# Moving taps of a convolution and chunks of a weight matrix about a block of attention steps

## The reference, cut to what matters

```python
q, k, v, qi, ki, wi, glu = jnp.split(rmsnorm(x, norm_mix_g) @ w_in, cuts, axis=-1)
a_out = dsa_attention(q, k, v, qi, ki, wi)      # 8 heads, 4 query blocks of 128, top-128 keys by an index score
ga, gg = jnp.split(glu, 2, axis=-1)
u = ga * jax.nn.sigmoid(gg)                     # 512 channels
u = causal_dwconv(u, conv_b_w, conv_b_b)        # 31 taps for each channel
b_out = jax.nn.silu(layernorm(u, ln_b_g, ln_b_b))
x = x + jnp.concatenate([a_out, b_out], axis=-1) @ w_out
m = rmsnorm(mem, norm_mem_g)                    # 256 memory rows
kc, vc = m @ w_k_cross, m @ w_v_cross           # keys and values of the later cross attention
```

## Time and profile before

| what | value |
|---|---|
| median of 3 runs | 1393.65 us (1391.83 to 1396.83) |
| time of the profiled execution | 1390.86 us |
| its span on the core | 1388.7 us |
| PE busy | 1337.5 us (96%) |
| DVE / ACT / POOL busy | 786.7 / 543.4 / 611.7 us |
| granted TensorE clock, mean | 0.99 |

### The profile page before, as it was taken

How to read it: one execution, slowest core, us unless ns; L and a number is a source line. 1 busy time by engine, 2 the same in 40 slices (tenths; PEclk the granted TensorE clock), 3 DMA queues, 4 the chain that set the end, 5 groups by cost and what they waited for, 6 DMA issues and landing times.

```text
span 1388.7 us, 18012 instructions
## 1 busy us (share of the span) xinstructions
PE 1337.5 (96%) x6189; PEld 1083.1 (78%) x6189; DVE 786.7 (57%) x1100; ACT 543.4 (39%) x855; POOL 611.7 (44%) x299
## 2 busy tenths in 40 slices
PE   7998989999999999999999998899999999999997
PEld 5787867787678888888888777677778888888887
DVE  6697897643456777777534588666453333332231
ACT  5454676543243322322223353444442322323322
POOL 4587974432244444444434533122344444444341
PEclk9999999999999999999999999899999999999999
DMA  6122321221122323223332222111122323223322
GB/s 224 46 91 90 114 70 47 76 92 61 46 76 92 105 91 98 98 91 108 104 104 79 89 78 74 46 47 46 61 91 93 104 91 101 95 96 106 103 84 82
DMA packets 31875, 121.19 MB, mean 87 GB/s; under 512 B 3536, under 2 KB 3664, under 8 KB 31568
## 3 DMA queue, kind: packets, MB, share of 16 engines
q1 hardware_dynamic: 31392, 119.55, 25.9%
q10 hardware_dynamic: 432, 0.96, 0.3%
HBM read 118.40 MB, written 2.10 MB: 87 GB/s over the span
## 4 chain that ended last, share of the span: by engine, by line
PE 73%; issue 13%; POOL 5%; DVE 5%; ACT 3%; DMA 1%; POOLq 0%; SPq 0%; ACTq 0%; DVEq 0%
PE acc L1701 60%; POOL weights_low L610 4%; PE acc L1838 3%; PE aux L2090 1%; PE acc L2186 1%; POOL conv L659 1%; PE aux L2070 1%; PE acc L1810 1%; DVE aux L1206 1%; PE aux L1924 1%; ACT weights_high L689 1%; DVE left L1551 1%; PE aux L2080 1%; DVE a_low L1367 1%; DMA weights_raw<-w 1%
## 5 line engine op out<-in xcount | busy, mean ns | idle before, releaser
L610 POOL TENSOR_TENSOR weights_low<-weights_raw,weights_high 128x1024 fp32r<-128x1024 f32 (+1 forms) x204 | 526.1, 2579 | 743.7 <-ACT weights_high L689 741.3
L689 ACT CAST weights_high<-weights_raw 128x1024 fp32r<-128x1024 f32 (+1 forms) x202 | 222.0, 1099 | 507.2 <-PE acc L1701 480.1
L1701 PE MATMUL acc<-a_high,weights_high 128*128 128x512 f32 x976 | 389.8, 399 | 4.5 <-POOL weights_low L610 3.1
L1701 PE MATMUL acc<-a_high,weights_low 128*128 128x512 f32 x976 | 381.1, 390 | 0.0
L1701 PE MATMUL acc<-a_low,weights_high 128*128 128x512 f32 x976 | 380.6, 390 | 0.0
L1701 PEld LDWEIGHTS acc<-a_high,weights_high 128*128 128x128 f32 x976 | 183.7, 188 | 47.0 <-issue 6.4
L1701 PEld LDWEIGHTS acc<-a_low,weights_high 128*128 128x128 f32 x976 | 183.8, 188 | 39.6 <-issue 2.6
L1701 PEld LDWEIGHTS acc<-a_high,weights_low 128*128 128x128 f32 x976 | 183.6, 188 | 38.5
L1179 DVE TENSOR_TENSOR residual<-acc,residual 128x512 f32<-128x512 f32 (+1 forms) x63 | 43.3, 687 | 172.0 <-PE acc L1701 129.8
L1701 PE MATMUL acc<-h_high,weights_high 128*128 128x512 f32 x330 | 129.0, 391 | 0.0
L1701 PE MATMUL acc<-h_high,weights_low 128*128 128x512 f32 x330 | 128.5, 389 | 0.0
(11 more groups left out here) (378 smaller groups left out, 1933.2 us busy)
## 6 DMA issues: line engine op xcount, KB each, us to landing
weights_raw<-w SPq DMA_DIRECT2D x172, 512.0 KB, 3.3
weights_raw<-w SPq DMA_DIRECT2D x32, 704.0 KB, 4.1
residual<-xT SPq DMA_DIRECT2D x8, 256.0 KB, 7.6
out<-y_tok SPq DMA_DIRECT2D x4, 512.0 KB, 3.1
mem_raw<-memT SPq DMA_DIRECT2D x1, 1024.0 KB, 5.4
mem_tok<-mem SPq DMA_DIRECT2D x1, 1024.0 KB, 7.4
lru_weights<-blockdiag ACTq DMA_DIRECT2D x1, 512.0 KB, 3.4
sine<-positions ACTq DMA_DIRECT2D x1, 256.0 KB, 7.0
```

Of the source, the lines that this page charges most:

```text
L610: g.tensor_tensor(weights_low[:, s, 0:cols], weights_raw[:, s, 0:cols], weights_high[:, s, 0:cols].bitcast(F32), ALU.subtract).then_inc(we ...
L689: a.copy(weights_high[:, s, 0:cols], weights_raw[:, s, 0:cols]).then_inc(weight_high, 1)
L1701: last = t_.matmul(acc[:, bank, 0:cols], w[:, s, wide], x_[:, k0 + k, 0:cols], start=start and k == opens and n == 0, stop=stop and k == c ...
```

## The change

No instruction is added or taken away; the same items stand in another order in `FIRST_PLAN`:

```diff
+        for n, first, end in ((12, 0, 2), (13, 2, 4), (14, 4, 7), (15, 7, 10)):
+            BETWEEN[n] += [("tap", i) for i in range(first, end)]
...
-        FILLS_AT = (2, 1, 2, 1, 2, 1, 2, 1, 1, 1, 2, 1, 1, 1, 1, 1, 1, 1, 0, 1, 1, 0, 1, 0,
-                    1, 0, 1, 0, 0, 1, 0, 0, 1, 0, 1)
-        CONV_STEPS, PRODUCT_STEPS = 31, 30
+        FILLS, HELD = FILLS[:23], FILLS[23:]
+        FILLS_AT = (1, 1, 1, 1, 1, 1, 1, 1, 1, 1, 1, 1, 1, 1, 1, 1, 1, 0, 1, 0, 1, 0, 1, 0,
+                    1, 0, 0, 1, 0, 0, 1, 0, 0, 0, 0)
+        LATE_TAPS = 12
+        CONV_STEPS, PRODUCT_STEPS = 33, 32
...
             if step < CONV_STEPS:
-                FIRST_PLAN += [("tap", i) for i in range(step * len(CONV) // CONV_STEPS,
-                                                         (step + 1) * len(CONV) // CONV_STEPS)]
+                rest = len(CONV) - 10 - LATE_TAPS
+                FIRST_PLAN += [("tap", 10 + i) for i in range(step * rest // CONV_STEPS,
+                                                              (step + 1) * rest // CONV_STEPS)]
...
-        FIRST_PLAN += [("mean",), ("heads_out", 3), ("centre",)] + FIRST[:2] + [("squares",)] + FIRST[2:4]
+        FIRST_PLAN += HELD[:2] + [("heads_out", 3)]
+        for n, item in enumerate(HELD[2:]):
+            FIRST_PLAN += [item] + [("tap", len(CONV) - LATE_TAPS + 2 * n + i) for i in range(2)]
+        FIRST_PLAN += [("mean",), ("centre",)] + FIRST[:2] + [("squares",)] + FIRST[2:4]
```

## The result

The changed kernel takes 1403.5 us in the median of 4 runs (1401.76 to 1405.56), the kernel before 1392.74 in 4 (1391.27 to 1396.83). The ratio is 1.0067, 95% interval 1.0051 to 1.0082: slower by 7.1 to 11.4 us. The profiled execution is the one of 1405.56 us. In it everything ahead of the change is already 1.5 us later than in the profile before (`glu 2` ends at 108.06, not 106.55). The two kernels are the same up to there. PE waits 2.8 us for a `weights_low` early on in both, and behind that wait the clock stays up in one profile and falls in the other.

The account below looks back on a forecast made before the run. The prediction saw DVE and PE waiting for each other, DVE giving the pace, and the front bound by when DVE reaches mask 0. It summed 9.2 − 14.3 + 13.7 = +8.6 us to 1402 us, range 1396 to 1408.5.

Parts of the forecast that it names:

- B: First to last mask: fewer halves and taps, so 81.8 us instead of 96.07, a gain of 14.3 us.
- C: Last mask to first half of w_out: held halves and taps make it 23.8 us instead of 10.1, +13.7 us.
- A, the taps ahead: Before the first mask: tap 0 waits 7.9 us for glu 2, so mask 0 comes 9.2 us later.
- with DVE giving the pace: First to last mask, kernel before: DVE, busy 84.16 of 96.07 us, and PE wait for each other; DVE paces.
- The rule weighed: PE waits in the tail: the page's throttling at each gap gives +10.2 us; the 1.66 us row, no clock loss, +8.6.
- Rival 1: First to last mask at PE's floor, 75.8 us: sum +2.6 us, 1396 us, no change that shows; chance 0.12.
- Rival 2: Steps wait as much as before, 86.4 us, and the tail's clock slows: +14.9 us, 1408.5 us; chance 0.18.
- Rival 3: Before the first mask: glu 2 ready for tap 0, mask 0 at 133.4, sum +0.8 us, 1394.5 us; chance 0.08.

Follow-up runs that it names:

- Experiment 4: Changed kernel with its first four taps moved ahead of the rotation of query 2: 1399.61 us against 1394.10 for the kernel before, ratio 1.0029.
- Experiment 1: Kernel before with only ten taps put ahead of the steps, the other 74 in the steps: 1402.81 us against 1394.10, ratio 1.0057.
- experiment 9: Kernel before with its 31 halves one in each of steps 0 to 30, no tap moved, nothing held: 1386.58 us against 1394.19, ratio 0.9943.
- 6: Changed kernel with heads_out 3 before the held chunks, five taps ahead where DVE idles: 1389.20 us against 1393.77 for the kernel before, ratio 0.9962.
- 2: Changed kernel without its taps ahead, 72 taps in the steps: 1396.40 us against 1394.10 for the kernel before, ratio 1.0015.
- experiment 7: Changed kernel with heads_out 3 before the held chunks and all 84 taps in the steps: 1393.09 us against 1393.77 for the kernel before, ratio 0.9995.
- Experiment 3: Changed kernel with heads_out 3 ahead of the first held chunk: 1398.04 us against 1394.10 for the kernel before, ratio 1.0027.
- 5: Changed kernel with no taps ahead and heads_out 3 before the held chunks: 1387.97 us against 1393.77 for the kernel before, ratio 0.9956.

## Why the prediction was right, and where it was not

The direction and the range held: +8.6 us forecast, +10.8 measured between the medians (7.1 to 11.4 by the interval), +9.8 by the marks. That the sum is off by only 1.2 by the marks is in part luck: B was 1.5 us too small a gain and C 2.9 us too small a loss, and they partly cancel. Term by term:

- **A, the taps ahead: +9.2 forecast, +9.0 read.** Tap 0 waits 7.75 us for `glu 2`, forecast 7.9; PE's stall is 10.15, forecast 10.6; the clock behind it is 0.54 for the 3 us from 143, as behind the stall of 3.43. Experiment 4 takes 5.9 us of the wait away and gets 4.5 us back by the marks; the six taps that find no idle time cost the other 4.5 of the 9.0.
- **B, the steps: −14.3 forecast, −15.8 read** (81.8 against 80.30 us). The size is right: PE is busy 74.1 us, forecast 74.6, and waits 6.2, forecast 7.2 with both ends. The reading of the kernel before is half wrong. I wrote of two engines "with DVE giving the pace". Experiment 1 takes ten taps out of that kernel and its steps are 1.9 us shorter; experiment 9 leaves all 84 in and they are 5.4 us shorter. With 21 halves, 58, 62, 67 and 78 taps between the first mask and the last (the change and experiments 6, 2 and 7) give 80.3, 80.4, 80.8 and 83.7 us. A share of 84 in 96 us busy did not mean that DVE was waited for at every step. Of B's 15.8 us, 9.6 are PE work that left, most of it the halves that come back in C, and 6.1 are less waiting (12.3 down to 6.2). The split of the waits was a guess: I gave POOL 3 us and `probT` 3, and they are 1.2 and 3.9.
- **C, the tail: +13.7 forecast, +16.6 read, the term that was mis-sized.** Three parts. `a_low` took 2.45 us, not 1.27. The taps took 9.4 from the end of `a_low`, not 9.0. And `mean` ran at half speed: PE's wait ahead of it was 4.09 us, not 2.8, and behind it the clock is granted at 0.53, so `mean` took 4.8 us instead of 3.44. Experiment 3 shows the chain that I gave: with `a_high` ahead of the cast there is no wait ahead of `mean`, no slow clock in the tail, and 6.0 us less. The clock was the term that I put at nothing.
- **The rule weighed** in the prediction, that a PE idling between bursts is throttled at each gap (the Trainium skill, TensorE: Matmul & The Clock Gate, "HAM oscillation — how this bites in real kernels"): of the two sums the page's (+10.2) was nearer here. After 4.09 us the clock fell to the level of 1.2 GHz; I had counted on a shorter wait and on the row of 1.66 us, behind which it stayed at 2.4. Neither rule is right as I used it. The kernel that the page tells of waits some 3 to 5 us each time, so "at each gap" was wider than what it says; the traces agree for 3.43 and 4.09 us, and not for 1.66. And my row of 1.66 us says little about 2.8: the kernel before has a wait of 2.85 us at 28.57, shown above, that I missed when I wrote that no row has one. The clock stays up behind it there, but falls behind the same wait in 9 of the 13 profiles.
- **Rival 1** (steps at PE's floor) had the steps at 75.8 us; they took 80.3. **Rival 2** had 86.4. **Rival 3** (taps ahead covered) is refuted by the 7.75 us.

What the prediction didn't see at all is that the waits in the steps were a matter of where the halves stand. Its rows had it: PE waited for `probT` at 188.16, in a step without a half, and 6.3 us in all. In experiment 9 it is 1.0 us.

Left open: why experiment 7 is 4 to 5 us behind 5. The two profiles show 3 us in the steps and 0.8 in the tail, spread over many short waits, and no run takes one of them alone. Open too is how much of 9's gain is the even spacing and how much is that the later steps hold more halves.

## What to carry to other kernels

Where work fills an engine's time between hand-overs, try one piece to each hand-over before anything else: here two pieces in some steps and none in others cost 6 to 10 us, and the share of busy time pointed at another engine. Moving whole pieces out of the loop only moves their time. Before an item goes ahead, look at when its input is ready: on an engine with a fixed order an early item is a wait for all that stands behind it. And where work is held back to cover something, follow the chain that starts the covered part; here one cast ahead of `a_high` kept the taps from starting until more than half of the cover was gone.

## What the runs showed of the hardware

The same `a_low` instruction takes 0.69, 1.27 or 2.45 us. Timeline of POOL beside it in the kernel before, then in the changed kernel:

```profile
235.05 2.35 POOL L610 TENSOR_TENSOR weights_low<-weights_raw,weights_high 128x1024 fp32r<-128x1024 f32 x1 [7.28 <-ACT weights_high L689]
```

```profile
232.21 2.38 POOL L618 TENSOR_TENSOR weights_low<-weights_raw,weights_high 128x1024 fp32r<-128x1024 f32 x1 [5.88 <-ACT weights_high L697]
```

Before, `a_low` starts at 236.68, POOL's subtraction ends at 237.40 and `a_low` at 237.95. In the changed kernel `a_low` starts at 232.69, POOL's ends at 234.59 and `a_low` at 235.14. In both it ends 0.55 us behind POOL's, whenever it began, and three more that begin beside a POOL add (at 193.16 and 217.49 before, at 191.07 in the changed kernel) end 0.55 us behind that add. So I read it as standing still until POOL's instruction is over, and not as slowed by a factor. In experiment 3 POOL has nothing to do beside it (229.71 to 230.40), and it takes 0.69. Both inputs of `a_low` lie in SBUF, and so do POOL's.

POOL is held up in turn when `a_low` is under way as its next instruction begins. In the kernel before, an earlier `a_low` runs to 172.01, and POOL's add beside it takes 1.74 us instead of its mean of 1.30:

```profile
171.42 1.74 POOL L659 TENSOR_TENSOR conv<-conv,product 128x512 f32<-128x512 f32 x1
```

The taps, which read their sum from PSUM and one tensor from SBUF, show nothing of the kind: eleven of them take 8.66 us, 0.79 each, although POOL subtracts beside several. That GpSimd and VectorE share SBUF interfaces and contend where a VectorE instruction has two SBUF inputs stands in the Trainium skill (GPSIMD Engine Reference, "1. Specifications"); the traces agree, with 0.58 and 1.76 us lost by `a_low`. So the engines meet not only at semaphores, as I wrote at the start: what one does in SBUF can hold up another.

Whether the clock falls behind a wait of PE changes from one execution to the next. The 13 profiles share three waits outside of this stage: behind 2.80 to 2.85 us (at 28.6) the clock fell in 9 of them, behind 2.86 to 2.88 us (at 991.6 in the kernel before) in 11, behind 1.84 or 1.85 us (at 864.4) in 7. Behind the waits of 1.63 to 1.69 us in the steps it stayed at 1.00 in all that have one. A single row on a short wait, as the prediction took it, can't say that the next one costs nothing.

Nor did the length of the wait set how long the clock stayed low. Behind 3.43 us it is 0.50 from 137 to 140. Behind 10.15 us it is 0.54 from 143 to 146 and 1.00 from 146 to 149 in the changed kernel, and 0.50 from 143 to 149 in experiment 3, whose instructions are the same up to there.
